# A mamba-2 layer inside a two-block fp32 kernel: another order for head weights, split weights and the first gate chunks

## The chip, the cores and the metric

One core of one Trainium2 chip runs the whole program in one launch. The metric is the device time of one execution, in microseconds (us). TensorE (PE) does the matrix products, VectorE (DVE), ScalarE (ACT) and GpSimd (POOL) the rest, and SyncE (SP) issues the loads of weights.

## The reference

The input is 256 tokens of width 1024. Two blocks follow each other, each of two layers. The first block is attention of four kinds and a hierarchical mixture of experts, the second is made of six sub-layers: a gated feed-forward, a mixer and a feed-forward, twice. The second layer's mixer is a mamba-2, and only that is touched by the change:

```python
proj = h @ w_in                                   # [256, 1024] x [1024, 5152]
z, xbc, dt = split(proj)                          # 2048, 3072, 32
xbc = silu(causal_conv4(xbc) + conv_b)            # depthwise, 4 taps
xs, B, C = split(xbc)                             # 32 heads x 64, 4 groups x 128, twice
dt = softplus(dt + dt_bias)                       # one step size a head
a = cumsum(dt * -exp(A_log))
w[t, s, h] = (C[t] . B[s]) * exp(a[t] - a[s])     # s <= t, per head
y = sum_s w[t, s, h] * dt[s] * xs[s, h]           # head output
y = (y + D * xs) * silu(z)
y = group_rms_norm(y) * norm_w                    # 4 groups of 512
out = y @ w_out                                   # [256, 2048] x [2048, 1024]
```

## The kernel before

All engines run one program each, in order, and meet by semaphores. Tokens lie on 128 partitions in two halves, called `tt` 0 and 1.

**Weights.** A weight matrix comes in pieces of 1 MB (128 x 2048) into a ring of three slots. `split_scalar` on ACT casts a piece to `w_hi` (fp32r), then `split_vector` on DVE writes the remainder to `w_lo` and so frees the ring slot (`raw_used`). Both have two buffers, so the high part of piece n waits until PE is done with piece n-2. `product` makes three matmuls of each: high x high, high x low, low x high. `split_next` in the mamba code is one such split, placed by hand in each engine's order; the high and the low split of a piece stand in two lists.

**PSUM.** There are eight banks. 0 and 1 (and 2 and 3) take the products of the projection, 4 to 7 the turned (transposed) chunks, by pairs; later 4 and 5 hold the rows of decays and 6 and 7 the outputs of two pairs of heads. Banks 2 and 3 are the side banks: they hold in turn scores, the turned x, and turned z. `side_used` counts their uses, and `SIDE` is their order.

**Projection.** `project_tensor` makes seven chunks (`MB_X`) of B, dt, C and x, of 512 columns each except dt. After a chunk, `behind` turns the one before it. ACT moves half 0 of a chunk to `staged`, DVE half 1 (`mamba_take`). Then DVE convolves the turned chunk (`conv(u)`, 12 instructions) on top of ACT's `first_tap(u)`, and ACT ends it with `silu(u)`.

**z and the output.** What is left of the weights is in 16 units of one piece, each of two halves (`half_unit(i, tt)`): 0 to 7 project z in four chunks q, two units each, and 8 to 15 are the output projection. Units 0 to 3 and 4 stand between `turn`, `scores` and `turn_x`; the chunks z 0 and z 1 are turned after unit 4 (`turn_z`) in banks 2 and 3, and ACT takes them with a silu (L2809).

**Heads.** 32 heads are treated as 16 pairs p. On PE, the loop does for pair p: `rows_of(p+2)` (L2679, decays as rows), `output(p)` (L2693, eight matmuls, waits for the weights of both heads), a `turn_z` at some p, one half unit where `FILL` says so (all p but 6 and 7), and `square_sums(p-4)` (L2705). ACT runs a pair ahead: `bounds(p+1)` (L2823), `exponentials(p+1)` (L2830), then `square_and_high(p-3)` and at the p of `SPLIT_IN` the high split of a unit. DVE does

```python
for p in range(20):
    if p < 16: weigh(2 * p)              # L2959: decays times scores, waits for the exponentials
    ...
    if 1 <= p < 17: skip(p - 1)          # L2963: waits for output(p-1)
    if p < 16: weigh(2 * p + 1)
    ...                                  # reduce, take_z, gate(p-3) (L2975), low(p-4) (L2979), add_out
    if p in SPLIT_IN: split_next()       # low split of the unit whose high split stands at this p
```

The weights of a head lie in `heads`, six buffers. Norms and the next feed-forward come after the last unit.

Of the kernel before, what the change touches and what calls it, by code (L numbers as in the profile page):

```python
# [23 lines left out]
SPLIT = 2  # L24
# [127 lines left out]
def build(nc, A, out):  # L152
# [18 lines left out]
    with ctx:  # L171
# [3 lines left out]
        def sem(name):  # L175
            return ctx.enter_context(nc.semaphore(name))
# [168 lines left out]
        side_used = sem("side_used")  # L345
        z_turned = sem("z_turned")
        z_ready = sem("z_ready")
        half_done = sem("half_done")
        sum_read = sem("sum_read")
        group_rooted = sem("group_rooted")  # L350
# [2139 lines left out]
        N_CONV = 6  # L2490
# [23 lines left out]
        PAIRS = ["chunk0", "sums"] + [f"chunk{u}" for u in range(1, N_CONV)]  # L2514
        pair_at = lambda name: 4 + 2 * (PAIRS.index(name) % 2)

        SIDE = ["bc0", "bc1", "xs0", "xs1", "xs2", "xs3", "z0", "z1", "z2a", "z2b", "z3a", "z3b"]


        FILL = {0: (5, 0), 1: (5, 1), 2: (6, 0), 3: (6, 1), 4: (7, 0), 5: (7, 1), 8: (8, 0), 9: (8, 1),  # L2520
                10: (9, 0), 11: (9, 1), 12: (10, 0), 13: (10, 1), 14: (11, 0), 15: (11, 1)}

        SPLIT_IN = {0: 6, 2: 7, 4: 8, 6: 9, 10: 10, 12: 11, 14: 12, 16: 13}

        def side_free(pe, name):
            if SIDE.index(name):
                pe.wait_ge(side_used, SIDE.index(name))

# [24 lines left out]
        def mamba_tensor(pe, t):  # L2553
            m_lhs = lambda b, tt: (MTh[:, b, tt * P:(tt + 1) * P], MTl[:, b, tt * P:(tt + 1) * P])

            def turn(u):
                name = f"chunk{u}"
                pe.wait_ge(proj_act, t.proj.at(1 if u == N_CONV - 1 else 0))
                pe.wait_ge(proj_dve, t.proj.at(1 if u == N_CONV - 1 else 0))
                pair_free(pe, name)  # L2560
                for i in range(4):
                    for tt in range(NT):
                        last = nc.tensor.transpose(turned_block(u, i)[:, tt * P:(tt + 1) * P],
                                                   staged[:, u % 2, tt, i * P:(i + 1) * P], ident[:, :])
                last.then_inc(conv_turned, 1)
# [15 lines left out]
            def scores(k):  # L2581
                pe.wait_ge(conv_done, 8)
                side_free(pe, f"bc{k}")
                for i in range(2):
                    g, b = 2 * k + i, 2 + i
                    Bg, Cg = feat[:, 16 + g, :], feat[:, 20 + g, :]
                    nc.tensor.matmul(ps[:, b, 0:S], Bg[:, 0:P], Cg, start=True, stop=True)
                    last = nc.tensor.matmul(ps[:, b, S:384], Bg[:, P:S], Cg[:, P:S], start=True, stop=True)
                last.then_inc(scored, 1)
# [49 lines left out]
            def unit(i):  # L2639
                half_unit(i, 0)  # L2640
                half_unit(i, 1)

            def behind(j):
                if j == DT:
                    turn(0)
                elif j == DT + 1:
                    sums()
                elif j > DT + 1:
                    turn(j - 2)

            project_tensor(pe, t, x_lhs, MB_X, arrived=x_arrived, behind=behind)
            z_first = t.proj.count
            scores(0)
            unit(0)
            turn(N_CONV - 1)
            scores(1)
            unit(1)
            turn_x(0)
            unit(2)
            turn_x(1)  # L2660
            unit(3)
            turn_x(2)
            half_unit(4, 0)
            turn_x(3)
            half_unit(4, 1)
            for q in range(2):
                side_free(pe, f"z{q}")
                turn_z(q, 0, 2)
                turn_z(q, 1, 3)

            def rows_of(p):

# [10 lines left out]
            def output(p):  # L2683

                pe.wait_ge(weights_ready, 2 * p + 2)
                if p < 2:
                    pe.wait_ge(pair_used[1], len(PAIRS) // 2)
                else:
                    pe.wait_ge(state_used, p - 1)
                for st, c0 in ((0, 0), (1, P)):  # L2690
                    for i in range(2):
                        h = 2 * p + i
                        last = nc.tensor.matmul(ps[64 * i:64 * i + 64, 6 + p % 2, c0:S],  # L2693
                                                xdt(h // 8)[:, st, (h % 8) * HD:(h % 8 + 1) * HD],
                                                weight(h)[:, st * S:st * S + S - c0], start=(st == 0), stop=(st == 1))
                last.then_inc(state_out, 1)

            def square_sums(p):
                pe.wait_ge(sq_ready, p + 1)
                if p == 0:  # L2700
                    pe.wait_ge(side_used, SIDE.index("z1") + 1)
                elif p % 4 == 0:
                    pe.wait_ge(sum_read, p // 4)
                for tt in range(NT):
                    last = nc.tensor.matmul(ps[:, 3, 16 * tt + p:16 * tt + p + 1],  # L2705
                                            gated_sq[:, p % 4, tt * P:(tt + 1) * P], ones[:, 0:1],
                                            start=True, stop=True)
                last.then_inc(sq_used, 1)

            rows_of(0)  # L2710
            rows_of(1)
            for p in range(16):
                if p < 14:
                    rows_of(p + 2)
                output(p)
                if p in (3, 4):
                    side_free(pe, "z2" + "ab"[p - 3])
                    turn_z(2, p - 3, 2)
                if p in (7, 8):
                    side_free(pe, "z3" + "ab"[p - 7])  # L2720
                    turn_z(3, p - 7, 2)
                if p in FILL:
                    half_unit(*FILL[p])
                if p >= 4:
                    square_sums(p - 4)
# [7 lines left out]
        def mamba_take(eng, tt):  # L2733

            move = nc.scalar.copy if tt == 0 else nc.vector.tensor_copy

            def take(j, src):
                if j == DT:
                    return move(tok32(dt_tok)[:, tt, :], src)
                u = chunk_of.index(j)  # L2740
                if u >= 2:
                    eng.wait_ge(conv_turned, u - 1)
                return move(staged[:, u % 2, tt, :], src)

            return take

        def take_z(eng, t, q, tt):

# [14 lines left out]
        def mamba_scalar(act, t):  # L2763
# [28 lines left out]
                split_scalar(act, t)  # L2792
                used(t)

            project_move(act, t, split_scalar, 0, MB_X, mamba_take(act, 0), behind=behind, more=2)
            t.first = t.piece.count
            t.add(pe_step=1, dve_step=1)
            split_next()
            first_tap(N_CONV - 1)
            take_z(act, t, 0, 0)  # L2800
            split_next()
            split_next()
            silu(N_CONV - 1)
            take_z(act, t, 1, 0)
            split_next()
            for q in range(2):
                for part in range(2):
                    act.wait_ge(z_turned, 2 * q + part + 1)
                    last = nc.scalar.activation(zT[:, 4 * q + 2 * part:4 * q + 2 * part + 2, :].rearrange("p b s -> p (b s)"),  # L2809
                                                ps[:, 2 + part, :], ACT.Silu)  # L2810
                last.then_inc(side_used, 1)
            act.wait_ge(mid_read, 1)
            act.wait_ge(z_turned, 4)

            def bounds(p):

# [53 lines left out]
        def mamba_vector(dve, t):  # L2870
# [67 lines left out]
                split_vector(dve, t)  # L2938
                used(t)

            project_move(dve, t, split_vector, 1, MB_X, mamba_take(dve, 1), behind=behind, more=2)
            t.first = t.piece.count
            scores(0)
            split_next()
            conv(N_CONV - 1)
            scores(1)
            take_z(dve, t, 0, 1)
            split_next()
            times_dt(0)
# [16 lines left out]
            def gate(p):  # L2966
                dve.wait_ge(state_used, p + 1)
                if p < 8:
                    dve.wait_ge(side_used, SIDE.index("z0") + 1 + p // 4)
                else:  # L2970
                    dve.wait_ge(z_ready, 1)
                if p >= 4:
                    dve.wait_ge(mt_high, p - 3)
                    dve.wait_ge(mt_ready, p - 3)
                TT(gated_y[:, p % 4, :], yT[:, p, :], zT[:, p, :], ALU.mult).then_inc(gated, 1)  # L2975
# [13 lines left out]
            def add_out(i, tt):  # L2989
# [10 lines left out]
                else:  # L3000
                    dve.wait_ge(out_added, 2 * (i - 10) + tt + 1)
                    STT(dst, src, group_root(g, tt), dst, ALU.mult, ALU.add).then_inc(out_added, 1)

            for p in range(20):
                if p < 16:
                    weigh(2 * p)
                if 10 <= p <= 16 and p % 2 == 0:
                    add_out(8 + (p - 10) // 2, 1)
                if 1 <= p < 17:
                    skip(p - 1)  # L3010
                if p < 16:
                    weigh(2 * p + 1)
                if p in (8, 12, 16):
                    reduce(p // 4 - 2)
                if p in (2, 6):
                    take_z(dve, t, 2 + p // 6, 1)
                if 3 <= p < 19:
                    gate(p - 3)
                if p >= 4:
                    low(p - 4)  # L3020
                if 9 <= p <= 15 and p % 2:
                    add_out(8 + (p - 9) // 2, 0)
                if p in SPLIT_IN:
                    split_next()
            split_next()
            add_out(12, 0)
# [184 lines left out]
```

## Time and profile before

| what | value |
|---|---|
| median of 3 runs | 2679.09 us (2678.89 to 2681.13) |
| profiled execution | 2679.62 us, its span 2677.8 us |
| busy | PE 84%, DVE 43%, ACT 31%, POOL 8% |
| granted TensorE clock, mean | 0.897 |
| HBM | 233 GB/s over the span |

The profile's span is taken from one execution. Times in the rows are us from its start. A bracket behind a timeline row is the idle time of that engine before it, and the instruction of another engine that ended it. A PE instruction's duration is longer than its distance to the next, since matmuls are pipelined.

### The profile page before, as it was taken

The numbers are of one execution on the slowest core, as the hardware profiler recorded it, in microseconds if no ns is written. First come the engines' busy times: TensorE is split into PE (matmuls) and PEld (weight loads), VectorE is DVE, ScalarE is ACT, GpSimd is POOL, SyncE is SP. The second block draws the span as 40 slices with busy tenths as digits, with TensorE's granted clock in tenths as the row PEclk, the third lists the DMA queues.
The fourth block names the chain that finished last, engine by engine and source line by source line (L and its number), as shares of the span: only waits on it lengthen the run. The fifth ranks groups of instructions, "written<-read, shape, count | busy, mean of one in ns | idle before, by whom it ended". The sixth has DMA issues, their size and how long they took to land.

```text
span 2677.8 us, 29253 instructions
## 1 busy us (share of the span) xinstructions
PE 2262.2 (84%) x10914; PEld 1548.2 (58%) x10914; DVE 1154.4 (43%) x1539; ACT 818.1 (31%) x1061; POOL 222.4 (8%) x259
## 2 busy tenths in 40 slices
PE   5969759997787876999869987479989989877998
PEld 5835444442674534343358866267867868655787
DVE  2454460000544544000055553345565567656555
ACT  2324320001232422000033333133333335564333
POOL 4000011111000001232110010010010010001000
PEclk9978779999797887999979988589989989988999
DMA  9566529998356553999845554035545545322553
GB/s 177 160 232 203 180 95 417 416 413 329 118 190 220 194 204 125 418 413 415 337 150 180 180 169 131 0 119 183 180 163 175 186 136 173 115 74 87 182 180 124
DMA packets 213822, 545.12 MB, mean 204 GB/s; under 512 B 25084, under 2 KB 52828, under 8 KB 188224
## 3 DMA queue, kind: packets, MB, share of 16 engines
q1 hardware_dynamic: 187456, 507.74, 53.0%
q0 software_dynamic: 18320, 22.55, 3.5%
q10 hardware_dynamic: 7920, 13.18, 1.4%
q8 instruction: 75, 1.23, 0.2%
q14 instruction: 51, 0.42, 0.0%
HBM read 611.92 MB, written 13.25 MB: 233 GB/s over the span
## 4 chain that ended last, share of the span: by engine, by line
issue 43%; PE 39%; DMA 6%; DVE 6%; POOL 2%; ACT 2%; DVEq 1%; POOLq 1%; ACTq 0%; SPq 0%
PE ps L1217 8%; PE ps L478 4%; PE ps L479 4%; PE ps L480 4%; PE ps L1240 4%; PE ps L1253 3%; DMA ring<-in_ada_w 2%; PE ps L932 2%; PE ps L1275 2%; PE ps L1202 2%; DMA ring<-in_w_in 1%; POOL rs L2171 1%; DMA proj<-in_w 1%; POOLq L2170 1%; DVE w_lo L456 1%
## 5 line engine op out<-in xcount | busy, mean ns | idle before, releaser
L456 DVE TENSOR_TENSOR w_lo<-ring,w_hi 128x2048 fp32r<-128x2048 f32 (+3 forms) x232 | 502.7, 2169 | 558.0 <-ACT w_hi L449 554.3
L449 ACT CAST w_hi<-ring 128x2048 fp32r<-128x2048 f32 (+3 forms) x232 | 418.9, 1808 | 685.8 <-PE ps L480 649.3
L478 PE MATMUL ps<-w_hi,XTh 128*128 128x512 f32 (+3 forms) x1344 | 522.7, 389 | 14.3 <-DVE w_lo L456 7.0
L479 PE MATMUL ps<-w_lo,XTh 128*128 128x512 f32 (+3 forms) x1344 | 516.6, 384 | 0.0
L480 PE MATMUL ps<-w_hi,XTl 128*128 128x512 f32 (+3 forms) x1344 | 515.7, 384 | 0.0
L478 PEld LDWEIGHTS ps<-w_hi,XTh 128*128 128x128 f32 x1344 | 260.0, 193 | 69.6 <-issue 15.9
L480 PEld LDWEIGHTS ps<-w_hi,XTl 128*128 128x128 f32 x1344 | 259.4, 193 | 50.3
L479 PEld LDWEIGHTS ps<-w_lo,XTh 128*128 128x128 f32 x1344 | 260.7, 194 | 47.1
L932 PE MATMUL ps<-ring,mid 128*32 128x512 f32 x576 | 106.7, 778 | 58.9 <-DMA ring<-in_ada_w 37.2
L478 PE MATMUL ps<-w_hi,hTh 128*128 128x512 f32 x320 | 125.0, 391 | 0.0
L480 PE MATMUL ps<-w_hi,hTl 128*128 128x512 f32 x320 | 124.6, 389 | 0.0
L479 PE MATMUL ps<-w_lo,hTh 128*128 128x512 f32 x320 | 124.6, 389 | 0.0
L1396 DVE TENSOR_TENSOR feat<-feat,ps 128x256 f32<-128x256 f32 x32 | 13.5, 421 | 223.4 <-ACT feat L1322 223.4
L1217 PE MATMUL ps<-moe_w,proj 128*64 128x512 f32 x416 | 93.8, 594 | 4.4 <-DMA moe_w<-in_w 2.4
L2212 PE MATMUL ps<-ident,Y 128*128 128x128 f32 x96 | 23.5, 425 | 84.9 <-DVE Y L2247 84.9
L1402 DVE COPY feat<-ps 128x256 f32<-128x256 f32 x32 | 13.6, 425 | 171.0 <-PE ps L1224 171.0
L1217 PE MATMUL ps<-moe_w,feat 128*64 128x512 f32 x384 | 86.7, 595 | 0.0
L2169 POOL TENSOR_SCALAR rs<-small 128x1 f32<-128x1 f32 x24 | 16.5, 686 | 845.6 <-ACTq L2164 845.0
L932 PEld LDWEIGHTS ps<-ring,mid 128*32 128x32 f32 x576 | 16.9, 126 | 117.7 <-DMA ring<-in_ada_w 70.1
L888 DVE SCALAR_TENSOR_TENSOR Y<-ps,Y 128x512 f32<-128x512 f32 x96 | 65.7, 688 | 33.7 <-PE ps L480 33.3
L1240 PE MATMUL ps<-moe_w,feat 128*64 128x512 f32 x352 | 79.6, 594 | 0.0
L653 PE MATMUL ps<-ident,X 128*128 128x128 f32 x64 | 15.4, 420 | 67.9 <-DVEq L774 38.9
(472 smaller groups left out, 2998.9 us busy)
## 6 DMA issues: line engine op xcount, KB each, us to landing
moe_w<-in_w SPq DMA_DIRECT2D x144, 1024.0 KB
ring<-in_ffn_w SPq DMA_DIRECT2D x128, 1024.0 KB, 5.1
ring<-in_ada_w SPq DMA_DIRECT2D x72, 1024.0 KB, 5.9
proj<-in_w SPq DMA_DIRECT2D x48, 1024.0 KB
ring<-in_w_in SPq DMA_DIRECT2D x32, 948.0 KB, 5.1
ring<-in_mb_w_in SPq DMA_DIRECT2D x20, 1024.0 KB, 5.1
ring<-in_ml_w_in SPq DMA_DIRECT2D x12, 1024.0 KB, 5.2
ring<-in_w_out SPq DMA_DIRECT2D x8, 1024.0 KB, 6.5
```

The lines of the kernel that those rows point to most:

```text
L449: nc.scalar.copy(w_hi[:, i, 0:n], ring[:, j, 0:n]).then_inc(hi_ready, 1)
L456: nc.vector.tensor_tensor(w_lo[:, i, 0:n], ring[:, j, 0:n], w_hi[:, i, 0:n].bitcast(F32), ALU.subtract).then_inc(raw_used, 1)
L478: nc.tensor.matmul(out, sh, mh, start=start, stop=False)
L479: nc.tensor.matmul(out, sh, ml, start=False, stop=False)
L480: return nc.tensor.matmul(out, sl, mh, start=False, stop=stop)
L888: nc.vector.scalar_tensor_tensor(yy, ps[:, 6 + tt, :], weight(tt), yy, ALU.mult, ALU.add).then_inc(y_used, 1)
L932: done_ = nc.tensor.matmul(ps[32 * j:32 * j + 32, 7, :], c_wide[:, feature, at_column:at_column + 32], piece[:, q, :], start=start, stop=stop)
L1202: last = nc.tensor.matmul(ps[:, 2 + j % 2, 0:n], x[:, tt, j, :], pick[:, g % 2, tt, 0:n], start=(tt == 0 and x is Xh), stop=(tt == NT - 1 ...
L1217: last = nc.tensor.matmul(ps[64 * hf:64 * hf + 64, f % 2, :], columns[:, j, :], w[:, :, c:c + 256], start=(j == 0), stop=(j == KD - 1))
L1240: last = nc.tensor.matmul(ps[64 * nh:64 * nh + 64, 6 + f % 2, :], hT[:, q, hf * 64:(hf + 1) * 64], fixed_w[u % 4][:, hf, c:c + 512], start ...
L1253: last = nc.tensor.matmul(ps[64 * hf:64 * hf + 64, 2 + m, 0:256], columns[:, j, :], over_w[n % 3][:, at_:at_ + 256], start=(j == 0), stop= ...
L1275: last = nc.tensor.matmul(ps[64 * nh:64 * nh + 64, 5, :], hT[:, q, hf * 64:(hf + 1) * 64], over_w[n % 3][:, c:c + 512], start=(hf == 0 and ...
```

## The change

1. DVE weighs one pair ahead: `weigh(0)` and `weigh(1)` stand before the loop, and turn p does `weigh(2p+2)` and `weigh(2p+3)`. `gate` comes one turn earlier (p-2), `take_z` and `add_out` move within the turn.
2. The low split of a unit stands one turn after its high split (`LOW_IN`), for the units 6 to 13.
3. z 0 and z 1 are turned in banks 6 and 7, z 0 right after unit 2 and z 1 after unit 3, and ACT takes them there (`early_z`, new semaphore `z_moved`). `SIDE` loses two entries. Unit 4 stands after `rows_of(1)`, with `turn_x(3)` between its halves.
4. The end of the projection is taken apart: `scores(0)` on PE stands before `turn(4)`, and DVE evicts it before `conv(4)`. The move of chunk 6 (`take_last`) stands after unit 0's high split and before `first_tap(4)` on ACT, and after `conv(4)` on DVE. Later splits of units 1 to 3 shift accordingly.

```diff
-        SIDE = ["bc0", "bc1", "xs0", "xs1", "xs2", "xs3", "z0", "z1", "z2a", "z2b", "z3a", "z3b"]
+        SIDE = ["bc0", "bc1", "xs0", "xs1", "xs2", "xs3", "z2a", "z2b", "z3a", "z3b"]
...
         SPLIT_IN = {0: 6, 2: 7, 4: 8, 6: 9, 10: 10, 12: 11, 14: 12, 16: 13}
+        LOW_IN = {p + 1: i for p, i in SPLIT_IN.items()}
...
@@ TensorE
                 elif j > DT + 1:
+                    if j == len(MB_X) - 1:
+                        pe.wait_ge(proj_act, t.proj.at())
+                        pe.wait_ge(proj_dve, t.proj.at())
+                        scores(0)
                     turn(j - 2)
...
-            scores(0)
             unit(0)
             turn(N_CONV - 1)
             scores(1)
             unit(1)
             turn_x(0)
             unit(2)
+            pe.wait_ge(pair_used[1], len(PAIRS) // 2)
+            turn_z(0, 0, 6)
+            turn_z(0, 1, 7)
             turn_x(1)
             unit(3)
             turn_x(2)
-            half_unit(4, 0)
-            turn_x(3)
-            half_unit(4, 1)
-            for q in range(2):
-                side_free(pe, f"z{q}")
-                turn_z(q, 0, 2)
-                turn_z(q, 1, 3)
+            pe.wait_ge(z_moved, 1)
+            turn_z(1, 0, 6)
+            turn_z(1, 1, 7)
...
             rows_of(0)
             rows_of(1)
+            half_unit(4, 0)
+            turn_x(3)
+            half_unit(4, 1)
...
+        def take_last(eng, t, tt):
+
+            eng.wait_ge(piece_done, t.piece.at(1 + SPLIT))
+            mamba_take(eng, tt)(len(MB_X) - 1, ps[:, tt, :]).then_inc((proj_act, proj_dve)[tt], 1)
+            t.add(proj=1)
+
@@ ScalarE
+            project_move(act, t, split_scalar, 0, MB_X[:-1], mamba_take(act, 0), behind=behind, more=2)
+            t.add(pe_step=1, dve_step=1)
+            split_next()
+            take_last(act, t, 0)
+            first_tap(N_CONV - 2)
+            split_next()
             t.first = t.piece.count
-            t.add(pe_step=1, dve_step=1)
             split_next()
             first_tap(N_CONV - 1)
             take_z(act, t, 0, 0)
             split_next()
             split_next()
             silu(N_CONV - 1)
+            early_z(0)
             take_z(act, t, 1, 0)
             split_next()
...
+            early_z(1)
@@ VectorE
+            project_move(dve, t, split_vector, 1, MB_X[:-1], mamba_take(dve, 1), behind=behind, more=2)
+            split_next()
+            scores(0)
+            conv(N_CONV - 2)
+            take_last(dve, t, 1)
+            split_next()
             t.first = t.piece.count
-            scores(0)
-            split_next()
             conv(N_CONV - 1)
             scores(1)
+            split_next()
             take_z(dve, t, 0, 1)
...
+            weigh(0)
+            weigh(1)
             for p in range(20):
-                if p < 16:
-                    weigh(2 * p)
-                if 10 <= p <= 16 and p % 2 == 0:
-                    add_out(8 + (p - 10) // 2, 1)
+                if p < 15:
+                    weigh(2 * p + 2)
                 if 1 <= p < 17:
                     skip(p - 1)
-                if p < 16:
-                    weigh(2 * p + 1)
+                if p < 15:
+                    weigh(2 * p + 3)
                 if p in (8, 12, 16):
                     reduce(p // 4 - 2)
+                if 2 <= p < 18:
+                    gate(p - 2)
+                if p >= 4:
+                    low(p - 4)
                 if p in (2, 6):
                     take_z(dve, t, 2 + p // 6, 1)
-                if 3 <= p < 19:
-                    gate(p - 3)
-                if p >= 4:
-                    low(p - 4)
-                if 9 <= p <= 15 and p % 2:
-                    add_out(8 + (p - 9) // 2, 0)
-                if p in SPLIT_IN:
+                if 9 <= p <= 16:
+                    add_out(8 + (p - 9) // 2, (p - 9) % 2)
+                if p in LOW_IN:
                     split_next()
```

## Rows read from the trace of the kernel before

**Rows 1.** The page, busy time: us, share of the span, instructions.

```profile
PE 2262.2 (84%) x10914; PEld 1548.2 (58%) x10914; DVE 1154.4 (43%) x1539; ACT 818.1 (31%) x1061; POOL 222.4 (8%) x259
```

**Rows 2.** Stages of the mamba sub-layer: us, busy (x count) by engine, granted clock, DMA.

```profile
2282.70:2334.80 52.10, 41.61 (x209) 33.61 (x207) 32.72 (x47) 25.23 (x42) 0.00 (x0) 0.95 0.37 122
2334.80:2433.90 99.10, 78.77 (x387) 58.83 (x387) 52.66 (x89) 62.53 (x130) 2.16 (x4) 0.85 0.22 75
2433.90:2460.80 26.90, 26.17 (x114) 21.02 (x113) 15.47 (x21) 9.01 (x11) 2.49 (x6) 0.94 0.36 118
```

**Rows 3.** Waits, 2334 to 2434: total us, times, longest.

```profile
PE ps L2693 <- DVE heads L2959: 22.7, 11, 4.9
...
DVE w_lo L456 <- ACT w_hi L449: 20.7, 7, 5.9
...
ACT temp L2836 <- DVE temp L2975: 20.4, 7, 4.2
...
ACT proj L2842 <- PE ps L2605: 8.6, 4, 4.1
```

**Rows 4.** Timeline of TensorE, 2282 to 2335: start, us, [idle before <-releaser].

```profile
2282.74 1.03 PE L2563 MATMUL ps<-ident,heads 128*128 128x128 f32 x8
...
2285.52 0.47 PE L478 MATMUL ps<-w_hi,XTh 128*128 128x512 f32 x1 [0.44 <-ACT heads L2743]
...
2295.14 0.67 PE L2587 MATMUL ps<-feat 128*128 128x256 f32 x2 [2.92 <-DVE masks L2917]
...
2304.55 1.06 PE L2596 MATMUL ps<-ident,feat 128*128 128x128 f32 x8 [0.67 <-DVE masks L2917]
...
2323.35 1.06 PE L2596 MATMUL ps<-ident,feat 128*128 128x128 f32 x8 [2.00 <-DVE proj L2923]
...
2328.82 1.09 PE L2605 MATMUL ps<-ident,heads 128*128 128x128 f32 x8 [0.74 <-ACT proj L2809]
...
2331.89 0.50 PE L2679 MATMUL ps<-decay_rows,pick_row 64*128 64x256 f32 x2 [1.32 <-ACT heads L2823]
...
2334.79 1.54 PE L2693 MATMUL ps<-heads,Y 128*64 128x256 f32 x8 [2.40 <-DVE heads L2959]
```

**Rows 5.** Timeline of TensorE at one pair of heads, and after a wait.

```profile
2345.59 0.50 PE L2679 MATMUL ps<-decay_rows,pick_row 64*128 64x256 f32 x2
...
2346.02 0.87 PE L2693 MATMUL ps<-heads,Y 128*64 128x256 f32 x8
...
2346.82 0.50 PE L478 MATMUL ps<-w_hi,XTh 128*128 128x512 f32 x1
...
2349.82 0.50 PE L2679 MATMUL ps<-decay_rows,pick_row 64*128 64x256 f32 x2
...
2364.28 1.55 PE L2693 MATMUL ps<-heads,Y 128*64 128x256 f32 x8 [3.28 <-DVE heads L2959]
```

**Rows 6.** Timeline of VectorE, 2285 to 2297.

```profile
2287.14 0.68 DVE L2743 COPY heads<-ps 128x512 f32<-128x512 f32 x1
2287.74 6.10 DVE L2883 SCALAR_TENSOR_TENSOR temp<-ps,conv_w,temp 128x255 f32<-128x255 f32 x12
2293.98 1.02 DVE L2917 SCALAR_TENSOR_TENSOR masks<-masks,ps 128x384 f32<-128x384 f32 x2
2294.91 2.29 DVE L456 TENSOR_TENSOR w_lo<-ring,w_hi 128x2048 fp32r<-128x2048 f32 x1
```

**Rows 7.** Groups by line and shape, 2334.8 to 2433.9: busy us, mean ns.

```profile
L2830 ACT ACTIVATE heads<-heads 128x384 f32<-128x384 f32 x30 | 14.1, 516 | 0.5
...
L2823 ACT ACTIVATE heads<-ps,small 128x256 f32<-128x256 f32 x29 | 13.6, 468 | 0.0
...
L449 ACT CAST w_hi<-ring 128x2048 fp32r<-128x2048 f32 x7 | 13.2, 1890 | 1.8 <-PE ps L480 1.8
...
L2860 ACT ACT_TABLE_LOAD x1 | 1.3, 1283 | 0.0
...
L2959 DVE TENSOR_TENSOR heads<-heads,masks 128x384 f32<-128x384 f32 x30 | 16.5, 552 | 1.3 <-ACT heads L2830 1.3
```

More of the change, by code:

```diff
@@ L347, in build @@
         z_ready = sem("z_ready")
+        z_moved = sem("z_moved")
         half_done = sem("half_done")
@@ L2686, in output @@
                 if p < 2:
-                    pe.wait_ge(pair_used[1], len(PAIRS) // 2)
+                    pe.wait_ge(z_moved, 2)
                 else:
@@ L2700, in square_sums @@
                 if p == 0:
-                    pe.wait_ge(side_used, SIDE.index("z1") + 1)
+                    pe.wait_ge(side_used, SIDE.index("xs3") + 1)
                 elif p % 4 == 0:
@@ L2793, in split_next, with early_z @@
                 used(t)
-            project_move(act, t, split_scalar, 0, MB_X, mamba_take(act, 0), behind=behind, more=2)
+            def early_z(q):
+                for part in range(2):
+                    act.wait_ge(z_turned, 2 * q + part + 1)
+                    last = nc.scalar.activation(zT[:, 4 * q + 2 * part:4 * q + 2 * part + 2, :].rearrange("p b s -> p (b s)"),
+                                                ps[:, 6 + part, :], ACT.Silu)
+                last.then_inc(z_moved, 1)
+            project_move(act, t, split_scalar, 0, MB_X[:-1], mamba_take(act, 0), behind=behind, more=2)
[4 more added lines that the diff above has]
+            split_next()
             t.first = t.piece.count
-            t.add(pe_step=1, dve_step=1)
             split_next()
@@ L2803, in mamba_scalar @@
             silu(N_CONV - 1)
+            early_z(0)
             take_z(act, t, 1, 0)
             split_next()
[L2806 to L2811, printed above, removed]
+            early_z(1)
             act.wait_ge(mid_read, 1)
-            act.wait_ge(z_turned, 4)
             def bounds(p):
@@ L2939, in split_next @@
                 used(t)
-            project_move(dve, t, split_vector, 1, MB_X, mamba_take(dve, 1), behind=behind, more=2)
+            project_move(dve, t, split_vector, 1, MB_X[:-1], mamba_take(dve, 1), behind=behind, more=2)
[4 more added lines that the diff above has]
+            split_next()
             t.first = t.piece.count
-            scores(0)
-            split_next()
             conv(N_CONV - 1)
             scores(1)
+            split_next()
             take_z(dve, t, 0, 1)
@@ L2968, in gate @@
                 if p < 8:
-                    dve.wait_ge(side_used, SIDE.index("z0") + 1 + p // 4)
+                    dve.wait_ge(z_moved, 1 + p // 4)
                 else:
```

## The prediction

> **What bounds the kernel now.** I read the page first: TensorE is busy 84% of the span [rows 1], so time is won only where it stands still or runs at its lower clock. Next the stages: of the three parts of the mamba sub-layer that the edits touch, the one of the head pairs is the loose one, 78.8 us busy in 99.1 at a mean granted clock of 0.85 [rows 2]. Then its waits: PE waited 11 times, 22.7 us, for VectorE's weighing (L2959), while VectorE waited 20.7 us for ScalarE's high parts, which stand in its queue ahead of the next pair's weighing [rows 3]. That is the mechanism to see: the low split blocks VectorE until PE has freed a buffer and ScalarE has cast into it, and only then are the weights made for which PE already stands.
>
> Last the timeline. A full turn of the pair loop takes 0.43 us for the rows of decays (2345.59 to 2346.02), 0.80 for the output, 3.00 for the half unit [rows 5]; square sums take the same 0.43 and a half-chunk turn about the same (my estimate from these rows). So the stage's work at the full clock is 16 x 0.80 + 14 x 0.43 + 14 x 3.00 + 12 x 0.43 + 4 x 0.42 = 67.7 us. Of the 99.1 us, 31.4 are loss: 22.7 - 2.4 = 20.3 of waits inside the stage (its first wait of 2.40 ends at its start [rows 3, 4]), and 11.1 that matmuls at the lower level cost. An output that follows a wait lasts 1.55 instead of 0.87 [rows 5]: after an idle stretch the granted clock is at 1.2 instead of 2.4 GHz. Six of the stage's waits, those of 2 us or more, are followed by such rows; 11.1 / 6 = 1.85 us is my price for one drop.
>
> **Part one, the end of the projection and the z units (52.1 us now).** Today's losses there: waits of 0.44, 2.92, 0.67, 2.00, 0.74, 1.32 and 2.40 [rows 4], 10.5 us, and one drop of 1.85 behind the 2.92 (the row of 0.67 us at 2295.14 is at the low level). Work: 39.7 us.
>
> Gone are: 0.44 (ScalarE now moves chunk 6 before it casts unit 1), 2.92 (the first scores are evicted before `conv(4)`, so the second find bank 2 free), 2.00 (`turn_x(3)` now stands half a unit and a z turn later), 0.74 (z is taken in banks of its own), 1.32 and 2.40 (unit 4's 6 us now lie over ScalarE's chain for the first pair: two silus, bounds, table load 1.28, exponentials [rows 7]). The output of pair 0 then finds its weights ready.
>
> New is a wait for VectorE's move of chunk 6. Now it is a copy of 0.68 at 2287.14, before `conv(4)` [rows 6]. After the change it stands behind it. PE ends chunk 6 at 2282.74, does scores and turn in the 2.3 us that both take now (to 2285.08), half 0 of unit 0 to about 2287.7, and half 1 waits for bank 1. VectorE: scores evicted 2284.1 to 2285.1; `conv(4)` can begin when ScalarE has made two first taps behind the later turn, about 2285.7; 6.10 us; the copy ends at 2292.6. PE waits 5.0 us, with one drop (half unit to 2297.5). Queued behind that half are `turn(5)`, the second scores and unit 1 (to 2305.2), and ScalarE's cast of unit 2, behind which the first taps of `conv(5)` stand: these come at 2299.5, `conv(5)` 2300.4 to 2306.5, scores evicted 2307.6, low part of unit 2 (2.29 us [rows 6]) 2309.8. So `turn_x(0)` waits 2.4 us and unit 2 another 1.2, with a second drop. Unit 2 begins some 4.5 us later than now. Sum: 39.7 + 5.0 + 2.4 + 1.2 + 2 x 1.85 = 52.0 us: this part gains nothing, but pair 0 starts at the full clock.
>
> Bounds of the new waits: nothing less than 4 us for the first (the convolution is 6.1 us and only 2.9 of unit 0's first half lie over it, from 0.9 us earlier), and no more than 7; the others between 0 and 5.
>
> **Part two, the pairs (99.1 us now).** I walked the queues with the durations of the rows: ScalarE needs for a pair 2.2 us of bounds and exponentials and 0.7 for square and high part, a cast 1.8 net, a z copy 0.5; VectorE 0.47 net for a head's weighing, 0.4 for each of skip, gate and low part, 2.2 net for a low split [rows 6, 7]. Pair p's weights are now made in turn p-1, and the low split stands behind two weighings and for a cast that ScalarE ended a turn ago. The waits of 20.3 and the six drops go, as long as ScalarE is ahead. In the walk PE reaches each output of pairs 1 to 6 after its weights, at a distance of 0 to 3 us. What is late next is ScalarE: between pairs 4 and 12 it is busy nearly all the time. My new waits are 1.0 at pair 7, 1.3 at pair 8 and 0.4 for the first group's sum, 0.6 for the first output bank at pair 11, and 2.5 before half unit 10 at pair 12 (the low part waits there behind exponentials that stand behind the late silu with its two table loads), with one drop. Sum: 67.7 + 5.8 + 1.85 = 75.4 us, 23.7 less than now.
>
> A table load is 1.28 us with no idle time before it, twice in the pair loop [rows 7]. By the Trainium skill (ScalarE: Activation LUTs, What ACT_TABLE_LOAD costs) a switch is 2.66 us with a drain; by that figure ScalarE would be 2.8 us later around pair 10 and the gain about that much smaller. The trace does not show the drain, so I don't add it.
>
> **Part three and the rest.** After pair 15 units 12 to 15 run at 26.2 us busy of 26.9 [rows 2]: nothing to win. Ring slots are freed a turn later, so SyncE's loads start later: in the walk the closest one is still issued over 15 us before its cast, so at three slots this costs nothing; without that lead it would be a load's time once.
>
> Sum: 0 - 23.7 us. The profiled execution took 2679.62 us (span 2677.8), 0.5 above the median of 2679.09; against the median this gives **2655 us**.
>
> **Rivals.**
> *ScalarE becomes the bound.* It is busy 62.5 us of the 99.1 now [rows 2] and waits 8.6 for turned z and 20.4 for gated y besides [rows 3]. Gating comes a turn earlier, so much of the 20.4 should go; if half stays in its chain, the stage cannot be shorter than 62.5 + 8.6 + 10.2 + 1.8 = 83 us. Gain 16: 2663. For it: the chain is in order and every turn's bounds wait for PE's rows. Against: most of its waits are for things that are earlier now.
> *The clock does not come back in part one.* If TensorE stays at 1.2 GHz from the 5 us wait until unit 1 has ended, 10.5 us of work take twice as long, less the 1.85 counted: 8.6 more, 2664. Against it: behind the wait of 2.92 the rows are full speed again within the next unit. The Trainium skill (TensorE: Matmul & The Clock Gate, Part 4: PE-mode transpose) says that transposes do not count as activity for the clock; the change puts one turn between the waits there, which by that rule could hold it low longer. No row here separates this.
> *No use.* The weights are late because of the exponentials, not because of the low split; then weighing earlier only moves the wait, and 2676 or so remains (pair 0's wait alone is won). Against it: VectorE waited for exponentials only 1.3 us inside the stage [rows 7].
> *Slower.* Low parts a turn later come too late for PE. That costs a wait like the one at pair 12, 2.5 + 1.85, at each of the seven pieces used between pairs 2 and 15: 67.7 + 7 x 4.35 + 3.3 = 101.5; with part one at the long end of its bound (2 more), 2683. It decides once PE reaches six of the seven half units before the subtraction ends. In the walk only one does; the others have 2 us or more.
>
> **How the numbers follow.** The forecast (2648 to 2659) has 0.54, ScalarE as the bound 0.18, the clock 0.10, better than forecast 0.08 (the new waits of part two don't come: 75.4 falls to 67.7, 2647), no use 0.05, slower 0.05. The range goes from 2647, that bound, to 2667, the two dearer cases with 3 us for the new waits of part one at their upper bounds; outside are no use, slower, and a little below. 0.2% is 5.4 us, about what a measurement of this kernel can tell from no change. Faster holds all but the last two: 0.90, same 0.05, slower 0.05.
>
> **What would show it.** In the profile after: at unit 0 a PE wait of about 5 us for VectorE's copy (L2743 or its new line), then about 2.4 and 1.2 around the first `turn_x`; no wait of a z turn for L2809; the first output without a wait and at the full clock. In the pairs: PE's waits for weighing down from 22.7 to below 4 us, those for the low part up from nothing to about 2.5, the stage near 75 us at a clock above 0.93, ScalarE busy over 80% of it. VectorE's waits for the high parts should nearly vanish. I am wrong if PE's waits move to L456 at several pairs, if exponentials end the weighing's wait in most turns, or if part one takes over 57 us.

## The result, and the profile after

The changed kernel takes 2651.55 us (median of 4 runs, 2650.47 to 2653.08), the one before 2678.99 in the same comparison: a ratio of 0.9897, 95% interval 0.988 to 0.9914. The forecast was 2655, with 2647 to 2667 as the range. The profiled execution has a span of 2651.3 us. Its three stages, as in [rows 2]:

```profile
2284.30:2336.70 52.40, 44.20 (x207) 35.30 (x205) 33.57 (x49) 26.79 (x46) 0.00 (x0) 0.90 0.36 121
2336.70:2409.10 72.40, 70.78 (x388) 53.75 (x387) 51.11 (x89) 61.27 (x129) 2.06 (x4) 0.93 0.26 88
2409.10:2433.40 24.30, 24.26 (x113) 19.68 (x113) 14.74 (x20) 8.16 (x9) 2.63 (x6) 1.00 0.51 172
```

| stage | before, us | after, us | forecast, us | PE's waits, before / after |
|---|---|---|---|---|
| one: end of chunk 6's products to the first output | 52.05 | 52.40 | 52.0 | 10.49 / 8.12 |
| two: to unit 12 | 99.10 | 72.35 | 75.4 | 20.34 / 1.62 |
| three: to the end of unit 15 | 26.9 | 24.3 | 26.9 | 0.60 / 0 |
| all else | 2499.8 | 2502.3 | 2499.8 | |

The last line is the span less the three stages. The edits don't touch that part; how much it scatters from one execution to the next is told below. By the three stages alone the change gains 29.0 us (178.05 to 149.05), where the forecast had 23.7.

**Stage one.** The timeline of PE, for [rows 4]:

```profile
2294.71 0.80 PE L479 MATMUL ps<-w_hi,XTh 128*128 128x512 f32 x1 [5.25 <-DVE heads L2750]
...
2310.81 1.70 PE L2598 MATMUL ps<-ident,feat 128*128 128x128 f32 x8 [2.46 <-DVE masks L2936]
...
2312.92 0.79 PE L479 MATMUL ps<-w_hi,XTh 128*128 128x512 f32 x1 [0.41 <-DVE w_lo L457]
...
2336.72 0.87 PE L2697 MATMUL ps<-heads,Y 128*64 128x256 f32 x8
```

and VectorE beside it, for [rows 6]:

```profile
2285.82 1.02 DVE L2936 SCALAR_TENSOR_TENSOR masks<-masks,ps 128x384 f32<-128x384 f32 x2 [0.85 <-PE ps L2590]
2287.64 6.12 DVE L2902 SCALAR_TENSOR_TENSOR temp<-ps,conv_w,temp 128x255 f32<-128x255 f32 x12 [0.81 <-ACT temp L2790]
2293.96 0.69 DVE L2750 COPY heads<-ps 128x512 f32<-128x512 f32 x1 [0.20 <-issue]
2294.57 2.28 DVE L457 TENSOR_TENSOR w_lo<-ring,w_hi 128x2048 fp32r<-128x2048 f32 x1
```

The copy of chunk 6 now stands behind the convolution, as its source line order says, and half 1 of unit 0 stands behind the copy. The waits of 0.44, 2.92, 0.67, 2.00, 0.74, 1.32 and 2.40 are gone, and 5.25, 2.46 and 0.41 have come. The output of pair 0 lasts 0.87 instead of 1.54: it is at the full clock.

**Stage two.** The waits, for [rows 3], with columns total us, times, longest:

```profile
DVE heads L2982 <- ACT heads L2849: 20.1, 8, 4.6
...
ACT temp L2855 <- DVE temp L2998: 0.8, 1, 0.8
PE ps L479 <- DVE w_lo L457: 0.8, 1, 0.8
PE ps L2697 <- DVE heads L2982: 0.8, 1, 0.8
```

Read both lists together. PE's wait for weighing fell from 22.7 us to 0.8. VectorE's wait for ScalarE's high parts, 20.7 us, is gone from the list altogether, and in its place VectorE now waits 20.1 us for the exponentials. This wait costs PE almost nothing (0.8 us, at pair 7), since it is for a pair that PE needs a turn later. ScalarE's wait for gated y fell from 20.4 to 0.8. ScalarE is busy 61.3 of 72.4 us.

What is left on PE in this stage is mostly the clock, around pairs 7 and 8. The granted clock is 0.50 from 2365.7 to 2375.9 and 1.00 in the rest of the stage:

```profile
2363.53 0.87 PE L2697 MATMUL ps<-heads,Y 128*64 128x256 f32 x8
...
2366.18 1.55 PE L2697 MATMUL ps<-heads,Y 128*64 128x256 f32 x8 [0.81 <-DVE heads L2982]
...
2370.06 1.55 PE L2697 MATMUL ps<-heads,proj 128*64 128x256 f32 x8
...
2376.84 0.50 PE L2709 MATMUL ps<-ones,temp 128*128 128x1 f32 x4
```

**Stage three.** Before, ScalarE's squares (L2836) of the last pairs came late, since they waited for VectorE's gates (L2975). PE waited for the squares, and the products behind that wait last 0.63 us instead of 0.40: it is one more drop of the clock.

```profile
2440.62 0.42 ACT L2836 ACTIVATE temp<-temp 128x256 f32<-128x256 f32 x1 [2.69 <-DVE temp L2975]
```

```profile
2441.09 1.33 PE L2705 MATMUL ps<-ones,temp 128*128 128x1 f32 x8 [0.60 <-ACT temp L2836]
...
2442.63 0.63 PE L479 MATMUL ps<-w_lo,MTh 128*128 128x512 f32 x1
...
2446.25 0.40 PE L479 MATMUL ps<-w_lo,MTh 128*128 128x512 f32 x1
```

After, the gates come a turn earlier, all 16 matmuls of the last sums run in one piece, and the clock stays at 1.00:

```profile
2414.72 1.84 PE L2709 MATMUL ps<-ones,temp 128*128 128x1 f32 x16
2416.42 0.48 PE L479 MATMUL ps<-w_hi,MTh 128*128 128x512 f32 x1
```

### The profile page after: what moved, and what is told of

Same layout as the page of the kernel before. It is cut to its first block, busy times and chain, and to the rows that moved or that the text cites. A ratio compares the mean times of both kernels' runs of the same rounds, so it can differ in the third digit from the quotient of the medians.

```text
span 2651.3 us, 29254 instructions
## 1 busy us (share of the span) xinstructions
PE 2256.7 (85%) x10914; PEld 1543.4 (58%) x10914; DVE 1151.6 (43%) x1539; ACT 817.6 (31%) x1061; POOL 222.6 (8%) x259
## 4 chain that ended last, share of the span: by engine, by line
issue 43%; PE 39%; DVE 6%; DMA 5%; DVEq 2%; POOL 2%; ACT 2%; POOLq 1%; ACTq 0%; SPq 0%
PE ps L1218 8%; PE ps L479 4%; PE ps L1241 4%; PE ps L480 4%; PE ps L481 4%; PE ps L1254 3%; PE ps L933 2%; DMA ring<-in_ada_w 2%; PE ps L1276 2%; DMA ring<-in_w_in 1%; PE ps L1203 1%; POOL rs L2172 1%; DMA proj<-in_w 1%; POOLq L2171 1%; PE ps L1735 1%
## 5 line engine op out<-in xcount | busy, mean ns | idle before, releaser
L1403 DVE COPY feat<-ps 128x256 f32<-128x256 f32 x32 | 13.6, 425 | 173.8 <-PE ps L1225 173.8
```

## The experiments

Executions of this program scatter. Of the same changed kernel one set of runs gave a median of 2651.55 and a second 2652.44, and the kernel before, run again beside each set, 2679 to 2683. The scatter sits in the part that no edit touches: the end of chunk 6's products came between 2274.6 and 2287.5 us after the start in the traces of the experiments. The three stages repeat far better: two traces of the changed kernel agree within 0.02 us in each, and two of end_new within 0.01. So each experiment is read from its stages first, and from its ratio second. The expectations are in us beside the first 2651.55. All stage lengths, in us, with PE's waits in brackets:

| kernel | one | two | three | median | ratio to before, interval |
|---|---|---|---|---|---|
| before | 52.05 (10.5) | 99.10 (20.3) | 26.9 | 2678.99 | 1 |
| changed | 52.40 (8.1) | 72.35 (1.6) | 24.3 | 2651.55 | 0.9897, 0.988 to 0.9914 |
| changed, second time | 52.38 (8.1) | 72.34 (1.6) | 24.3 | 2652.44 | 0.9883, 0.9868 to 0.9899 |
| low_back | 52.34 (8.1) | 71.66 (2.8) | 24.3 | 2646.56 | 0.9864, 0.9846 to 0.9883 |
| weigh_back | 52.35 (8.1) | 75.09 (6.0) | 26.2 | 2655.10 | 0.99, 0.9883 to 0.9916 |
| both_back | 52.35 (8.1) | 96.00 (20.5) | 28.5 | 2680.72 | 0.9992, 0.9978 to 1.0006 |
| z_back | 60.29 (14.3) | 75.69 (2.9) | 24.3 | 2659.28 | 0.9914, 0.9898 to 0.993 |
| end_back | 45.66 (4.0) | 72.30 (3.3) | 24.3 | 2647.13 | 0.987, 0.9855 to 0.9885 |
| copy_first | 44.76 (3.1) | 73.88 (2.9) | 24.3 | 2648.13 | 0.9865, 0.9849 to 0.9882 |
| end_new | 39.50 (0.4) | 72.31 (3.2) | 24.3 | 2637.11 | 0.9834, 0.982 to 0.9847 |
| end_new, second time | 39.50 (0.4) | 72.31 (3.1) | 24.3 | 2638.85 | 0.9839, 0.9826 to 0.9853 |
| end_low | 39.52 (0.4) | 71.27 (2.7) | 24.3 | 2635.70 | 0.9817, 0.98 to 0.9834 |
| hole_split | 52.36 (8.1) | 76.48 (5.4) | 24.3 | 2655.56 | 0.9898, 0.9882 to 0.9915 |

All but the first are the changed kernel with the edit told below. low_back, weigh_back, z_back and end_back undo one part of the change each, both_back two.

### Which edit of the pair loop pays

**The low split back beside its high split (low_back).**

```diff
-                if p in LOW_IN:
+                if p in SPLIT_IN:
                     split_next()
```

> The changed kernel (2651.6 us) with one edit undone: VectorE's low split of a unit stands again in the same turn as ScalarE's high split; weighing stays a pair ahead. Theory 1 (either edit alone is enough: with weights a pair ahead the blocked queue is covered, because ScalarE's next exponentials stand behind the same cast and are what VectorE would wait for anyway): 2651 to 2655, PE's waits for weighing below 4 us. Theory 2 (the low split's place is the edit that pays): the old waits behind the cast come back, 2662 or more, PE waiting over 8 us for weighing.

**The weighing back in its own turn (weigh_back).** The body of VectorE's loop is the old one, but for the low split.

```diff
-            weigh(0)
-            weigh(1)
             for p in range(20):
-                if p < 15:
-                    weigh(2 * p + 2)
+                if p < 16:
+                    weigh(2 * p)
...
-                if 2 <= p < 18:
-                    gate(p - 2)
+                if 3 <= p < 19:
+                    gate(p - 3)
...
                 if p in LOW_IN:
                     split_next()
```

> The changed kernel (2651.6 us) with the other edit undone: a pair is weighed in its own turn again, with the old order of VectorE's turn; the low split stays a turn later. Theory 1 (either edit alone is enough, but in the short turns 6 and 7, which hold no half unit, PE's 1.7 us are less than VectorE's skip, two weighings and gate, so waits of about 1 us come back there): 2654 to 2658. Theory 2 (the low split's place is what pays): 2651 to 2654. Theory 3 (weighing ahead is what pays): 2662 or more.

**Both back (both_back).** The two diffs above together.

> The changed kernel (2651.6 us) with both of these edits undone; unit 4, the z chunks and the end of the projection stay as changed. All theories that give the 26.7 us of the pair loop to VectorE's order: the waits of 20.3 us and five drops of the clock come back, the loop takes 97 instead of 72.4 us, 2676. If unit 4 and the z chunks had given much of it: below 2668.

The three belong together with the changed kernel: a square of two edits. With both undone stage two takes 96.0 us and stage three 28.5. The low split a turn later alone takes them to 75.1 and 26.2, weighing ahead alone to 71.7 and 24.3, the two together to 72.35 and 24.3. Either breaks the queue and gives most of the gain. Beside weighing ahead the later low split has nothing left to give, its stage two is even 0.7 us longer. Beside the later low split weighing ahead still gives 4.6 us. Weighing and gates moved together in this edit, and no run parts them.

Theory 1 of low_back and weigh_back holds by the waits and the stages, and theories 2 and 3 fall; the median of low_back, 2646.56, lies below its 2651 to 2655. Not foreseen in weigh_back were three waits of 0.93 to 1.36 us at pairs 10, 12 and 14; those at pairs 7 and 8, 0.37 and 1.91, were. The ratio of 0.9992 puts both_back at 2676.9 us beside the 2678.99 of before, where 2676 was expected (its own runs have 2680.72 beside 2681.93). Nearly all of the change's gain is in this pair of edits, and the other two come out at 1.2 us together by the stages.

The waits of both_back show the old pattern, and those of weigh_back what the low split's place does by itself (total us, times, longest):

```profile
PE ps L2697 <- DVE heads L2982: 20.5, 10, 4.9
DVE w_lo L457 <- ACT w_hi L450: 19.3, 7, 5.9
```

```profile
PE ps L2697 <- DVE heads L2982: 5.5, 5, 1.9
...
DVE w_lo L457 <- ACT w_hi L450: 1.7, 2, 1.3
```

In low_back the wait for the cast is back in VectorE's queue, 5.5 us in 4 waits, yet PE pays only one wait of 1.91 for weighing:

```profile
DVE heads L2982 <- ACT heads L2849: 12.7, 6, 4.6
DVE w_lo L457 <- ACT w_hi L450: 5.5, 4, 2.5
...
PE ps L2697 <- DVE heads L2982: 1.9, 1, 1.9
```

The exponentials that VectorE needs next stand behind the same cast in ScalarE's queue, so what it waits longer for the cast it waits less for them (20.1 became 12.7).

### Unit 4 and the early z

**The z chunks turned after unit 4 again (z_back).** Unit 4 and the z chunks go back together, so this run doesn't part the two.

```diff
             unit(2)
-            pe.wait_ge(pair_used[1], len(PAIRS) // 2)
-            turn_z(0, 0, 6)
-            turn_z(0, 1, 7)
             turn_x(1)
             unit(3)
             turn_x(2)
-            pe.wait_ge(z_moved, 1)
-            turn_z(1, 0, 6)
-            turn_z(1, 1, 7)
+            half_unit(4, 0)
+            turn_x(3)
+            half_unit(4, 1)
+            for q in range(2):
+                side_free(pe, f"z{q}")
+                turn_z(q, 0, 2)
+                turn_z(q, 1, 3)
...
             rows_of(1)
-            half_unit(4, 0)
-            turn_x(3)
-            half_unit(4, 1)
```

> The changed kernel (2651.6 us) with the third edit undone: z 0 and z 1 are turned after unit 4 in banks 2 and 3, unit 4 stands before the rows of pair 0. Theory: the waits of 2.00, 0.74, 1.32 and 2.40 us return with one drop of 1.85 us, 8.3 us in all: 2660. Rival: these waits were only pushed there by what came before, and unit 4 covers nothing that another engine would not have finished: within 3 us of 2651.6.

PE's timeline has four waits of the kernel before again, 2.00, 0.74, 1.32 and 2.12 (was 2.40) us:

```profile
2329.73 1.94 PE L2598 MATMUL ps<-ident,feat 128*128 128x128 f32 x8 [2.00 <-DVE proj L2941]
...
2336.76 1.09 PE L2607 MATMUL ps<-ident,heads 128*128 128x128 f32 x8 [0.74 <-ACT proj L2809]
...
2339.83 0.78 PE L2684 MATMUL ps<-decay_rows,pick_row 64*128 64x256 f32 x2 [1.32 <-ACT heads L2841]
...
2342.73 1.55 PE L2698 MATMUL ps<-heads,Y 128*64 128x256 f32 x8 [2.12 <-DVE heads L2981]
```

Stage one is 7.9 us longer, and stage two 3.3: the drop around the first output reaches into it, and a wait of 2.13 for a low part, with a drop, stands instead of 0.81. That is 11.2 us by the stages; its median lies 7.7 and 6.8 us above the two of the changed kernel. The theory holds, the rival falls. In stage one this edit gives 7.9 us, about what the fourth, next, costs.

### The end of the projection

**The old end of the projection (end_back).** ScalarE's order goes back as well; its lines are left out here.

```diff
-                    if j == len(MB_X) - 1:
-                        pe.wait_ge(proj_act, t.proj.at())
-                        pe.wait_ge(proj_dve, t.proj.at())
-                        scores(0)
                     turn(j - 2)
...
+            scores(0)
             unit(0)
...
-            project_move(dve, t, split_vector, 1, MB_X[:-1], mamba_take(dve, 1), behind=behind, more=2)
-            split_next()
-            scores(0)
-            conv(N_CONV - 2)
-            take_last(dve, t, 1)
-            split_next()
+            project_move(dve, t, split_vector, 1, MB_X, mamba_take(dve, 1), behind=behind, more=2)
             t.first = t.piece.count
+            scores(0)
+            split_next()
             conv(N_CONV - 1)
             scores(1)
-            split_next()
             take_z(dve, t, 0, 1)
```

> The changed kernel (2651.6 us) with the fourth edit undone: the end of the projection as before (first scores after the last turn, chunk 6 moved before the last but one convolution, old places of the splits); z and unit 4 stay as changed. My sum: PE's waits of 5.25, 2.46 and 0.41 us with two drops go (11.8 us), 0.44, 2.92 and 0.67 with one drop return (5.9 us): 2645.7, faster than the changed kernel. Rival: the fourth edit is needed for the early z turn, and later waits take the 5.9 us back: 2651 or more.

Stage one is 6.7 us shorter than the changed kernel's, 0.8 more than expected. Its waits in that stage:

```profile
PE ps L2589 <- DVE masks L2929: 2.9, 1, 2.9
PE ps L2598 <- DVE masks L2929: 0.7, 1, 0.7
PE ps L479 <- ACT heads L2747: 0.4, 1, 0.4
```

Stage two is no longer than the changed kernel's, so the rival, that later waits take the gain back, falls. Beside the other three, the fourth edit makes the kernel slower.

**Chunk 6 moved before the convolution (copy_first).**

```diff
             scores(0)
-            conv(N_CONV - 2)
             take_last(dve, t, 1)
+            conv(N_CONV - 2)
             split_next()
```

> The changed kernel (2651.6 us) with one line moved: VectorE moves chunk 6 before the convolution that now stands ahead of it. Theory: the wait of 5.25 us and its drop go; new waits of 1.6 us (low part of unit 1), 1.6 (second scores) and 1.3 (low part of unit 2); unit 2 begins 7.6 us earlier: 2644. Rival: PE only waits for the convolution elsewhere (turn or scores), gain under 3 us: 2649 to 2652.

```profile
2299.41 0.50 PE L479 MATMUL ps<-w_hi,XTh 128*128 128x512 f32 x1 [1.80 <-DVE w_lo L457]
...
2307.04 1.06 PE L2598 MATMUL ps<-ident,feat 128*128 128x128 f32 x8 [0.23 <-DVE masks L2936]
...
2309.15 0.50 PE L479 MATMUL ps<-w_hi,XTh 128*128 128x512 f32 x1 [1.04 <-DVE w_lo L457]
```

The wait of 5.25 is gone. The three expected ones have come, 1.80, 0.23 and 1.04 us instead of 1.6, 1.6 and 1.3, and stage one is 7.6 us shorter. Stage two gives 1.5 of that back (a wait of 2.04 for the low part of unit 10 instead of 0.81).

**A new order (end_new).**

```diff
@@ ScalarE
             take_last(act, t, 0)
-            first_tap(N_CONV - 2)
             split_next()
+            first_tap(N_CONV - 2)
@@ VectorE
             scores(0)
-            conv(N_CONV - 2)
             take_last(dve, t, 1)
             split_next()
             t.first = t.piece.count
-            conv(N_CONV - 1)
+            conv(N_CONV - 2)
             scores(1)
             split_next()
             take_z(dve, t, 0, 1)
-            split_next()
             times_dt(0)
+            split_next()
+            conv(N_CONV - 1)
```

> The changed kernel (2651.6 us) with the end of the projection in a new order. VectorE: low part of unit 0, first scores, move of chunk 6, low part of unit 1, conv(4), second scores, low part of unit 2, z 0, x 0, low part of unit 3, conv(5); ScalarE casts unit 1 before the first taps of conv(4). Theory: nothing that PE needs stands behind a 6 us convolution any more, all three waits and both drops go: part one falls from 52.4 to about 40.5 us, 2640. Rival: the last convolution now comes 5 us later and PE waits for its silu at the last turned x, or for unit 4's low part: 2644 to 2648.

```profile
2278.30:2317.80 39.50, 39.12 (x209) 32.30 (x207) 33.38 (x49) 26.82 (x46) 0.00 (x0) 1.00 0.49 161
```

VectorE's timeline of it, all that PE needs ahead of each long convolution:

```profile
2280.69 0.68 DVE L2750 COPY heads<-ps 128x512 f32<-128x512 f32 x1
2281.29 2.28 DVE L457 TENSOR_TENSOR w_lo<-ring,w_hi 128x2048 fp32r<-128x2048 f32 x1
2283.49 6.11 DVE L2902 SCALAR_TENSOR_TENSOR temp<-ps,conv_w,temp 128x255 f32<-128x255 f32 x12
2289.74 1.02 DVE L2936 SCALAR_TENSOR_TENSOR masks<-masks,ps 128x384 f32<-128x384 f32 x2
2290.68 2.28 DVE L457 TENSOR_TENSOR w_lo<-ring,w_hi 128x2048 fp32r<-128x2048 f32 x1
...
2296.07 2.28 DVE L457 TENSOR_TENSOR w_lo<-ring,w_hi 128x2048 fp32r<-128x2048 f32 x1
2298.27 6.10 DVE L2902 SCALAR_TENSOR_TENSOR temp<-ps,conv_w,temp 128x255 f32<-128x255 f32 x12
```

PE has one wait of 0.38 us in the whole stage, the granted clock is 1.00, and the stage takes 39.5 us. Its rival, a late wait for the last convolution's silu, did not come.

### The drop at pairs 7 and 8

**The two turns without a half unit parted (hole_split).**

```diff
-... 4: (7, 0), 5: (7, 1), 8: (8, 0), ...
+... 4: (7, 0), 6: (7, 1), 8: (8, 0), ...
```

> The changed kernel (2651.6 us) with unit 7's second half in turn 6 instead of 5, so that the two turns without a half unit (5 and 7) are no longer neighbours. It asks for the drop of the clock at pair 7, which followed a wait of only 0.81 us. Theory activity (the stretch of short matmuls lowers the clock, not the wait): the drop goes or shortens and up to 4 us are won: 2647.5 to 2650. Theory wait: PE meets the same wait at pair 7 and the same drop, or one more for z: 2651.5 to 2654.

```profile
2358.51 1.25 PE L2697 MATMUL ps<-heads,Y 128*64 128x256 f32 x8 [1.12 <-DVE heads L2982]
...
2367.21 0.50 PE L2683 MATMUL ps<-decay_rows,pick_row 64*128 64x256 f32 x2 [0.81 <-ACT heads L2842]
...
2369.22 1.55 PE L2697 MATMUL ps<-heads,proj 128*64 128x256 f32 x8 [1.51 <-DVE heads L2982]
...
2392.18 0.50 PE L479 MATMUL ps<-w_hi,MTh 128*128 128x512 f32 x1 [2.00 <-DVE w_lo L457]
```

Stage two is 4.1 us longer. The low level did not go, it now shows after both of the parted turns (outputs of 1.25 and 1.55 us) and behind the wait of 2.00. The stage's granted clock is 0.93 as before this edit, and PE's waits rose from 1.6 to 5.4 us, which is 3.8 of the 4.1. The activity theory's gain did not come. By the stages the result is 2655.7, beyond the 2651.5 to 2654 of the other theory. Which of wait and thin work lowers the clock there is not settled.

### The three side by side

**The changed kernel again (changed_rerun)**, without an edit.

> The changed kernel itself, beside the next two on one chip, since single executions of this program scatter by a few us between chips. 0.989 to 0.991 of before; its pair loop 72.4 us and part one 52.4 us as in its first trace if waits are what repeats.

**The new end again (end_new_rerun)**, the same kernel as end_new.

> The new order of the projection's end once more, beside the changed kernel. By the stages of its first trace (39.5 and 72.3 us against 52.4 and 72.4): 12.9 to 13.1 us faster than the changed kernel, 0.983 to 0.985 of before.

**The new end with the low splits beside the high ones (end_low)**, the diffs of end_new and low_back together.

> The new end of the projection, and the low splits back in the turn of their high splits. If the second edit of the change adds nothing once weighing is a pair ahead: the same as the new end alone within 1 us in the pair loop (71.7 to 73 us). Rival: without the slack that the slow part one gave to ScalarE, the low split waits for the cast again in the first turns, over 75 us.

On one chip they took 2652.44, 2638.85 and 2635.7 us. The new end is 13.6 us faster than the changed kernel by medians and 12.9 by stages. The second edit adds nothing here either (stage two takes 71.3 us without it, 72.3 with it), and the rival of over 75 us did not come. The interval of end_low overlaps that of end_new, so between these two no order is claimed; both beat the changed kernel and the one before.

## Why the prediction was right

The mechanism was right in the main, and the sum missed by 3.5 us on the side of caution. By the stages it missed by 5.3 (154.3 against 149.05); that the total is nearer is luck, the scatter of the part that no edit touches. By its own terms:

- **Part one: nothing gained, pair 0 at full clock.** Forecast 52.0, measured 52.40. The wait for the copy was put at 5.0 (5.25), the one for the second scores at 2.4 (2.46), the one for unit 2's low part at 1.2 (0.41: the turn before it ran at the low level and took 1.70 instead of 1.06, so PE came later). Two small errors cancel: the waits, put at 8.6, are 8.1, and the two drops, put at 3.7, leave 4.6. The runs z_back and end_back show that this part holds a gain and a loss of about the same size: unit 4 and early z give 7.9 us here, the fourth edit takes 6.7.
- **Part two: PE's waits for weighing go.** Forecast 75.4, measured 72.35. The work term was 67.7; eight of the 14 half units, those of the output projection, take 2.89 us instead of 3.00 (2401.69 to 2404.58), which is 0.9 less. The waits were put at 5.8 and are 1.62: at pair 8 and 11 none came, at pair 12 the low part was late by 0.81 instead of 2.5. The clock was put at one drop of 1.85, and what is left of the stage, 72.35 - 66.8 - 1.6, is 3.9 us. It is one drop, at pair 7 instead of pair 12, and longer. The price of 1.85 was a mean over unequal drops: in the kernel before, too, one of the six was long, with the granted clock at 0.50 from 2374.3 to 2384.5, around pair 7.
- **The step that was off: part three, "nothing to win".** It had lost 2.6 us: a wait of 0.60 us for the last squares and a drop behind it, hidden in a stage that looked 97% busy. A busy share counts slow matmuls as busy; the granted clock of 0.94 in the same row of [rows 2] was the hint. both_back (28.5 us) and low_back (24.3) differ only in VectorE's order of weighing and gates, so it is that order, with its gates a turn earlier, that won it.
- **The rivals.** ScalarE did not become the bound: its wait for gated y fell to 0.8 us, where the rival kept half of 20.4. It is the busiest after PE, though, at 85% of the stage. The clock came back within a half unit and the turn behind it: the granted clock is 0.50 up to 2300.8, inside that turn, and 1.00 from there, and the second scores already run in 0.60 us, as the first do (0.59). The Trainium skill (TensorE: Matmul & The Clock Gate, Part 4: PE-mode transpose) says that transposes don't count as activity; by that rule the clock might have stayed low longer. Here the 12 products of a half unit stood ahead of the turn, and the trace does not separate the two. "No use" was half seen: exponentials end the weighing's wait in 8 of the 15 turns, 20.1 us. That is most turns, which the prediction had named as a sign of being wrong. The sign came without the loss, since with a turn in hand PE feels only 0.8 us of it: the sign was badly chosen. "Slower" needed six late low parts and got one.
- **Table loads.** Both loads of the stage again took 1.28 us and the next instruction followed at once (load at 2376.22, next at 2377.52). The Trainium skill (ScalarE: Activation LUTs, What ACT_TABLE_LOAD costs) puts a switch at 2.66 us with a drain; this trace does not show the drain.

What the prediction took as one change is two that pay and one that costs, with one that is idle: the edit of the low split adds nothing beside the weighing (without it stage two is 0.7 us shorter), and the fourth edit costs 6.7 us in stage one. The prediction priced that loss inside its sum but did not say that the edit should be left out.

## What to carry to other kernels

Put nothing on an in-order queue ahead of work that another engine waits for, if the thing ahead has itself to wait or is long: ahead of the copy the 6 us convolution cost 5.25 us of PE, and in end_new, behind the copy, the first scores and the low part, it cost nothing. When two edits loosen the same queue, one of them may do it all: run each alone. Read the granted clock beside the busy share, and measure stages by their first and last instruction when whole executions scatter more than the edit is worth.

## What was not expected of the hardware

The drop of the clock at pairs 7 and 8 does not follow from the length of a wait alone. In the changed kernel it begins at 2365.7, in the wait of 0.81 us ahead of the output of pair 7. In end_new the same output stands behind the same wait and is at full clock, and the drop begins 2.2 us after that output's start, ahead of pair 8:

```profile
2347.21 0.87 PE L2697 MATMUL ps<-heads,Y 128*64 128x256 f32 x8 [0.81 <-DVE heads L2982]
2348.64 0.63 PE L2607 MATMUL ps<-ident,temp 128*128 128x128 f32 x4 [0.55 <-DVE temp L2773]
...
2351.06 1.55 PE L2697 MATMUL ps<-heads,proj 128*64 128x256 f32 x8 [0.63 <-DVE heads L2982]
```

In the kernel before, waits of 0.94, 1.05 and 1.36 us had no such rows behind them. In both_back even one of 2.46 us, ahead of pair 11, had none: the granted clock is 1.00 from 2389 to 2416. So the length of a wait by itself tells neither that a drop comes nor that none does. All the kernels have the drop in this stretch, where two turns hold no half unit; hole_split did not remove it by parting them, and no run here separates thin work from short waits as its cause.
